# Unread products on TensorE ahead of and between the transposes of the latents' rows

## The reference, cut to what matters

```python
h_lat = modulate(rmsnorm(x_lat, norm_mix_pre[layer]), sh1[:, None], sc1[:, None])
...
def s5_scan(u, lam_bar, b_bar, s0, reverse):
    bu = jnp.einsum('btgh,gph->btgp', u, b_bar)
    first = -1 if reverse else 0
    bu = bu.at[:, first].add(lam_bar * s0)
    a = jnp.broadcast_to(lam_bar, bu.shape)
    _, states = lax.associative_scan(_lin_rec_combine, (a, bu), axis=1, reverse=reverse)
    return states
...
y_lat = y_lat + jnp.einsum('btgp,ghp->btgh', st_lat, c_mat).real
...
z = jax.nn.gelu(y.reshape(h.shape).astype(h.dtype))
a, g = jnp.split(z @ w_glu, 2, axis=-1)
```

## Time and profile before

| | |
|---|---|
| median of 3 runs | 2633.77 us |
| lowest and highest | 2629.77 and 2634.45 us |
| span of the profiled execution | 2631.6 us |
| PE busy | 2410.6 us, 92% |
| DVE busy | 1789.8 us, 68% |
| ACT busy | 1050.7 us, 40% |
| mean DMA rate | 266 GB/s |
| mean granted clock of PE | 0.941 |

### The profile page before, as it was taken

The page is one execution under the profiler, slowest core; times in us unless marked ns, Lnnn a source line. Parts: engine busy times, 40 slices in busy tenths (PEclk is TensorE's granted clock), DMA queues, the critical chain, the costliest instruction groups (busy, mean ns, idle before and its releaser), DMA issues.

```text
span 2631.6 us, 42442 instructions
## 1 busy us (share of the span) xinstructions
PE 2410.6 (92%) x17791; PEld 2017.8 (77%) x17791; DVE 1789.8 (68%) x2871; ACT 1050.7 (40%) x1588; POOL 176.1 (7%) x290
## 2 busy tenths in 40 slices
PE   5699999899789899989999686899799999999998
PEld 1488887677656698779887485688698998998986
DVE  4647779688766766877897648577654677554555
ACT  0243334354552323343663222444444443443443
POOL 1101333111100000211000000000000000000000
PEclk7799999899889999989999857999899999999999
DMA  9969998699678769979768887688455678655553
GB/s 352 337 230 348 367 342 284 197 355 347 254 280 292 267 246 342 385 274 321 254 228 324 261 319 294 239 272 276 147 185 192 216 272 282 222 179 191 191 164 109
DMA packets 317518, 699.75 MB, mean 266 GB/s; under 512 B 13648, under 2 KB 14160, under 8 KB 312464
## 3 DMA queue, kind: packets, MB, share of 16 engines
q1 hardware_dynamic: 298496, 627.29, 69.2%
q0 software_dynamic: 18560, 67.66, 7.1%
q10 hardware_dynamic: 272, 2.10, 0.2%
HBM read 646.78 MB, written 56.49 MB: 267 GB/s over the span
## 4 chain that ended last, share of the span: by engine, by line
PE 74%; DVE 13%; DMA 9%; ACT 3%; issue 1%; SPq 0%; POOL 0%; DVEq 0%; ACTq 0%
PE bank L2279 71%; DVE arena L1424 3%; DMA ring<-in_w_mod 3%; DVE sm L1424 2%; DVE ring_lo L1424 2%; PE bank L2282 1%; DVE LT L1432 1%; DMA ring<-in_a_w_in 1%; DMA ring<-in_kv_w 1%; DVE arena L1432 1%; DMA ring<-in_b_w_out 1%; PE bank L2567 1%; DMA arena<-in_ctx 1%; DMA ring<-in_b_w_in 1%; DMA arena<-arena 1%
## 5 line engine op out<-in xcount | busy, mean ns | idle before, releaser
L1424 DVE TENSOR_TENSOR ring_lo<-ring,w_hi 128x1024 fp32r<-128x1024 f32 (+1 forms) x380 | 427.5, 1133 | 342.4 <-ACT w_hi L1017 332.2
L1017 ACT CAST w_hi<-ring 128x1024 fp32r<-128x1024 f32 x316 | 330.2, 1048 | 470.4 <-PE bank L2279 468.4
L1017 ACT CAST att_w_hi<-ring 128x1024 fp32r<-128x1024 f32 x192 | 197.3, 1048 | 327.7 <-DMA ring<-in_kv_w 118.4
L1424 DVE TENSOR_TENSOR ring_lo<-ring,att_w_hi 128x1024 fp32r<-128x1024 f32 x192 | 233.7, 1221 | 127.3 <-ACT att_w_hi L1017 126.0
L2279 PE MATMUL bank<-in_hi,w_hi 128*128 128x256 f32 x1024 | 288.8, 282 | 1.1 <-ACT n L964 1.1
L2279 PE MATMUL bank<-in_lo,w_hi 128*128 128x256 f32 x1024 | 288.9, 282 | 0.0
L2279 PE MATMUL bank<-in_hi,ring_lo 128*128 128x256 f32 x1024 | 288.5, 282 | 0.0
L2279 PE MATMUL bank<-w_hi,hid_lo 128*128 128x512 f32 x640 | 256.7, 401 | 3.3 <-DVE ring_lo L1424 3.3
L2279 PE MATMUL bank<-att_w_hi,att_hi 128*128 128x512 f32 x512 | 210.3, 411 | 14.2 <-DVE ring_lo L1424 14.2
L2279 PE MATMUL bank<-ring_lo,att_hi 128*128 128x512 f32 x512 | 204.5, 399 | 0.0
L2279 PE MATMUL bank<-att_w_hi,att_lo 128*128 128x512 f32 x512 | 203.9, 398 | 0.0
(11 more groups left out here) (278 smaller groups left out, 5096.5 us busy)
## 6 DMA issues: line engine op xcount, KB each, us to landing
ring<-in_w_mod SPq DMA_DIRECT2D x192, 1024.0 KB, 9.5
ring<-in_a_w_in SPq DMA_DIRECT2D x64, 1024.0 KB, 8.1
ring<-in_w_mlp_in SPq DMA_DIRECT2D x64, 1024.0 KB, 5.3
ring<-in_w_mlp_out SPq DMA_DIRECT2D x64, 1024.0 KB, 5.1
ring<-in_kv_w_mod SPq DMA_DIRECT2D x32, 1024.0 KB, 10.6
ring<-in_kv_w SPq DMA_DIRECT2D x32, 1024.0 KB, 8.0
ring<-in_b_w_in SPq DMA_DIRECT2D x32, 1024.0 KB, 5.6
ring<-in_s_w_glu SPq DMA_DIRECT2D x32, 1024.0 KB, 5.3
```

What stands on the lines that cost most here:

```text
L1017: a.copy(whi(h), raw_half(h)).then_inc(*o.up("whi"))
L1424: return v.tensor_tensor(dst, x, y, op).then_inc(*(to or o.up("dve")))
```

## The change

A function `warm(n)` issues n products of `ident` (128 x 128, as weights) with 96 columns of `sel`, into columns 416 to 511 of bank 7, which nothing reads and nothing else writes at that time. They have no wait and tell no semaphore. 50 of them run between the last `sums` of the stretch and the first transpose of the latents' rows, and 2 behind each of the 8 groups of 16 transposes; the last 2 stand ahead of the wait for `u_made`. Nothing is removed, and no other engine's program changes.

```diff
@@ -2415,6 +2415,11 @@
+            def warm(n):
+
+                for _ in range(n):
+                    mm(MB0[:, 416:512], ident[:, :], sel[:, 0:96], True, True)
+
@@ -2696,8 +2701,10 @@
                 mod(j)
             u_sums(1)
             sums(MOD_AT_TURN[-1])
+            warm(50)
             for pc in range(8):
                 u_turn(1, pc)
+                warm(2)
             p.wait_ge(S["u_made"], 16)
```

## The result

The kernel after takes 2642.43 us (median of 20 runs, 2636.74 to 2651.52), the kernel before 2633.36 (20 runs, 2629.44 to 2641.68). The ratio is 1.0035, with an interval of 1.0028 to 1.0043: 9 us slower (7.4 to 11.3). The forecast of 2634 and the range up to 2639 miss it. The profiled execution of after has a span of 2639.8 us and took 2641.61.

A forecast was written before the change was run, and what follows sets the result against it. It took the copying of the f = 0 half of the v products to set the end. +0.9 us for the start and -0.8 for the remainder at full speed made +0.1, giving 2634 us; range 2620 to 2639.

The forecast's parts named there:

- The frame: The kernel's end moves with the moment at which the f = 0 half of the v products is copied.
- Part 1: 50 products, 100 records, in PE's pause before the transposes: clock rises after 3 to 7 us; transposes start 1.1 us late.
- the price by columns: Low-end price of an added product's record if its 96 columns set the pace: 0.16 at half clock, 0.083 at full.
- Part 2: Eight transpose groups, two products behind each, at full clock: 1.6 us a group, -0.2 us in all (-1.2 to +0.9).
- rival 3: Clock rises in the pause, then is lost among the transpose groups, cold groups 2.5 us each: +6.1 us, 2640; chance 0.08.
- Part 3: The pause before the v products loses the clock; v runs as before, save a remainder at full speed worth 0.8 us.
- the last pause: PE's remaining pause of about 1.2 us between the transposes and the v products, expected to lose the clock.
- rival 1: Clock holds over the pause before v, whose first 512 records take 15.1 us instead of 27.4: 2622 us; chance 0.22.

The follow-up runs named there:

- the fastest kernel: Kernel before plus wide unread products: five behind the last transpose group, nine ahead of the first readout, seven ahead of the second; 2626.57 us, ratio 0.9981.

## Why the prediction was wrong

**The frame held.** What counts is when the f = 0 half of v is copied: with v as cold as before, 7.44 us more ahead of it are 7.5 more at the second readout.

**Part 1 held.** The rise came 3.6 us behind the first product (3 to 7, middle 5); in the kernels with four products behind each group and with the 50 alone it came after 5.0 and 6.7. The 100 records took 13.10 us (13.4): 73 took 8.00 us at 1.00 in 1508 to 1516, 0.110 each, where the weights had given 0.111; 0.083, the price by columns, is refuted. The first transpose came 15.58 us behind the sums against 15.03: 0.55 late, where I had 1.1; in the two others it is 1.20 and 2.03.

**Part 2 failed, in its clock.** Its price at 1.00 was right: groups 1517.77 - 1516.05 = 1.72 us apart (1.45 to 1.75). But only two of eight were worked at it. The forecast let 1.00 stand through all eight and fall in the pause behind them. The third took 2.41, four took 2.94 each, and the last one's transposes 1.84: 2 x 1.72 + 2.41 + 4 x 2.94 + 1.84 = 19.45 us (1516.05 to 1535.50), where before has 12.63. 0.55 + 6.82, and 0.07 more in the pause ahead of v, make the 7.44.

**The step behind it is the dismissal of rival 3 on the earlier trace rows.** There 16 transposes of 128 x 128 were PE's last work, and the clock was still 1.00 4 us later. I read this as "transposes keep the clock", for transposes of any size. The Trainium skill ("TensorE: Matmul & The Clock Gate", Part 4: PE-mode transpose) says that transposes don't count as busy for the clock. For the groups here, of 32 rows, the traces agree (lost after 2.4 us of them alone, lost in the third group with two or four narrow products between and in the fourth with two wide ones); for 128 x 128 the run with 64 of them disagrees, 7.15 us at 1.00. I had used a true row for a shape that it doesn't show. It was also a thinner row than I took it for: PE stood idle in it, and the first idle microseconds keep 1.00 by themselves, as the 2.4 to 5.2 us above show. The row that did bear on it, the first run's groups at 1.00 with six wide products behind each, has three times the work between groups that this change has.

**Rival 3 was under-sized too.** Its path was the right one, with two groups at full clock and the rest cold. But it had 2.5 us for a cold group where the trace has 2.94, since the cold transposes were taken at the 0.099 they cost in a row of 128; between products 16 of them take 1.84 us, not 1.6, and the four records 1.10, not 0.84 and a change of 0.06. Its groups came to 17.3 us, the trace's to 19.45. I had +6.1, the stretch has +7.4.

**Part 3 was not put to the test by the change,** since v was reached cold, with the clock lost long before the last pause that I had weighed. But its argument that v is too light for 1.00 was wrong: 55 us at 0.50 in the earlier trace rows show that v doesn't raise the clock, not that it doesn't keep it. Where the clock was up at v's start or rose within its first 1.6 us, it stayed up for 10 to 17 us of v, and fell in a pause of PE or up to 2.1 us behind one; that the pause is what ended it wasn't tried. The 12.3 us of rival 1 were out of reach all the same: the best first half was 20.7 to 21.0 us up to DVE's first step and not 15.1 + 1.06 = 16.2. In the profile with 21.0, 3.1 us of the rest are PE's pauses at full clock (below), and 1.5 us are the 127 records among which the clock falls (5.40 us instead of 3.92).

**The chance** of 0.08 for rival 3 was the expensive number. Against it stood one row of another shape.

**Open:** the 1.6 us of the median beyond the stretch (a later rise in the pause would give it, as the 0.65 and 1.5 us more of lateness in the two other profiles show, but one profile doesn't tell what the other executions did); the scatter with wide products among the groups, which goes with the granted clock; why the two products alone cost 5.8 us in time and 9.8 in their profile; and which part of the fastest kernel brings its gain, since neither alone can be told clearly from nothing.

## To carry to other kernels

Before work is added to keep the clock up, look for a row in which the very shape that lies between keeps it: small transposes kept PE busy and lost it, and each filler among them was then paid at half speed. The place to try filler is one where a pause covers it and the next work on the path is long and can keep the clock by itself (here right ahead of v and of the second readout). Even there the gain was small: only both together (0.9981) and one of two occasions of five products (0.9987) were clear of noise. That a kind of work never raises the clock doesn't say that it can't hold it.

## What the runs showed that I had not expected

**Rise and hold are different things.** v products without a gap stay at 0.50 for 55 us in before; in the kernel with five products ahead they stay at 1.00 for 17 us (1537.3 to 1554.4), over two short pauses. What differs is what ran just ahead of them.

**At full clock PE stops at fixed places of its instruction stream.** The v products at 1.00 stop every 127 or 128 records for 0.6 to 2.6 us, with nothing that the profile shows to wait for. In the four profiles with five or seven products the first pause is behind 267 to 271 records, the second 127 further. Where v is cold from its start there is none; in the first profile with five products two more stand behind the fall, the one at 1558.60 and one at 1566.53. The same pieces stand in the readouts of before (1651.55, 1658.69). The places move with what is added: with four records more ahead (seven products instead of five) the first pause comes four v records earlier, 267 instead of 271, and with 68 more (the kernel with 22 wide products in the pause) it comes at 331, which is 271 - 68 + 128. So they lie on a grid of 128 records in all that PE is given, which with their weight loads are 256 instructions. The Trainium skill ("Runtime: NRT & Kernel Launch", Instruction fetch mechanics) has the instructions fetched in blocks of 256 and calls the cost mostly hidden. The block fits; the cost is not hidden here. The page of before has the fetches as a queue:

```profile
q8 instruction: 141, 2.31, 0.3%
```

2.31 MB in 141 packets are 16.4 kB each, 64 bytes for each of 256 instructions. The trace also has when each packet went, and PE starts again 2.3 to 2.7 us behind one, in each of the fifteen pauses that were read: in the kernel with five products packets at 1543.8, 1550.0, 1556.1 and 1564.2 and restarts at 1546.30, 1552.46, 1558.60 and 1566.53; in before packets at 1649.1, 1656.3 and 1662.2 and restarts at 1651.55, 1658.69 and 1664.90. In the cold v of before the packets come as well (1542.0, 1548.7) and PE doesn't stop: 128 records last 3.9 us at full clock and 6.85 at half. So the pauses are waits for the next block, as far as times and places can show it. Why the packets come late isn't known. Around these pauses in v the data transfers hold the DMA engines near 1.00 (0.95 to 1.02 over the records between them), but behind the packet of 1662.2 the restart took 2.7 us with the DMA engines at 0.00 from 1663.6 on; nothing was tried by moving the transfers.

**The length of a pause is a poor sign.** 1.48 us ahead of the first group and 1.79 and 2.25 us inside v were followed by a fall, and 2.61 us ahead of the second readout by none. The section of the Trainium skill that the prediction cites on idle gaps ("TensorE: Matmul & The Clock Gate", Why this matters for your kernels) warns of gaps above about 3 us only; all four are shorter, and three were followed by a fall. The first of the three had small transposes behind it, which lose the clock without any pause.
